# Latent attention over paged keys: pages turned in 32x32 blocks on VectorE, scores on 32-row quarters of TensorE

## The chip, the cores and the metric

One core of a Trainium2 chip runs the whole program. The metric is the device time of one execution in microseconds. Three runs of the kernel before gave 3005.11, 3011.60 and 3019.53; the median is 3011.6. One more execution was recorded by the profiler.

## The reference, cut to what matters

A decoder layer, twice: feed-forward, three mixers side by side (a recurrence, a dilated window attention, a latent attention), feed-forward. 256 prompt tokens and 8 samples of 8 new tokens each pass through it. Everything is float32. The change is in the third mixer, for the samples. Each of them has 2048 past positions in a paged cache of 128 positions a page: 256 latent numbers and 32 rotary numbers a position. 8 heads x 8 tokens make 64 queries a sample, all on the same keys.

```python
def latent_attention(q_lat, q_rope, ckv_all, krope_all, q_off):
    scale = (DNOPE + DROPE) ** -0.5
    ...
        s = (jnp.einsum('bqhc,blc->bhql', ql, ckv_all)
             + jnp.einsum('bqhr,blr->bhql', qr, krope_all)).astype(jnp.float32) * scale
        s = jnp.where(key_rows[None, :] <= rows[:, None], s, -jnp.inf)
        p = jax.nn.softmax(s, axis=-1)
        return jnp.einsum('bhql,blc->bqhc', p.astype(ckv_all.dtype), ckv_all)
```

## The kernel before

The program is written engine by engine, and each engine runs its list in order. Semaphores (`S["..."]`) join the lists. The order around the change is written out by hand in a function `ml_sample` of three engines; nothing schedules it. Transposes have line 654 and matmuls line 651 in the profile, since two helpers issue them.

A sample's pages come by indirect DMAs that GpSimd issues (lines 633 and 636): one for the rotary part (`KRr`) and two for the latent part (`KRc`, 8 positions to a partition in each half). Four buffers hold four samples. Sample 0 is loaded long before; samples 1 to 3 are issued as the stage begins; sample b + 3's are issued when values(b - 1) has raised `ml_pv`.

Positions lie in partitions, which is right for the product with the shares but not for the scores, where channels must lie there. So TensorE turns every 128x128 piece (`transposed`, groups of four), nine groups a sample, into two PSUM banks; ScalarE empties the even ones (line 1626) and VectorE the odd ones (line 2180) into `KTl` and `KRT`. `scores` then contracts 128 channels at a time. The 64 queries fill half of the array's columns, so two halves of the keys go side by side (`r` = 0, 1). `QL` holds the latent queries, `QRz` the rotary ones, four times with zeros around. The scores of a sample fill two PSUM banks, of two pairs that take turns.

Then, per sample: VectorE finds the maximum over PSUM (`maximum`, line 2191 is the large one of 128x1024), ScalarE takes exponentials (`exponentials`, lines 1636 and 1637), TensorE turns the shares (`shares`, 8 pieces of 128x128 and a small one), VectorE copies them out (`shares_out`, lines 2217 and 2218), TensorE multiplies them with the pages (`values`, 8 pairs and a last small product), ScalarE copies the result (line 1647), and `by_channel` turns it while dividing. `own_tokens` scores the 8 new tokens. TensorE's loop weaves these steps of samples b, b - 1 and b - 2 between the transposes of the next half.

`prompt_branch` is the last projection of the prompt's part of this mixer, in 8 tiles with weights ("br", "c") that SP loads when `ml_pv` is 6. Those of `w_out` ("wo") follow. They fill the end of the stage. Before the stage stands `ml_prompt`, which ends with `prompt_y`.

Of the kernel before, what the change touches and what calls it, by code (L numbers as in the profile page):

```python
# [175 lines left out]
TAIL_BANK = (4, 5, 0, 1, 2, 3, 7, 6)  # L176
# [44 lines left out]
def weight_slots(units):  # L221
# [24 lines left out]
    "latent_root", "lora_g", "lora_wa", "lt_T", "lt_act", "lt_dve", "masked", "prods", "q_ev", "series", "state", "t_ev", "vb", "x2_ev", "xp", "y_out", "logs", "mixed", "ml_PT", "ml_done",  # L246
    "ml_exp", "ml_mm", "ml_nm", "ml_oT", "ml_olT", "ml_osb", "ml_own", "ml_div", "ml_p", "ml_prep", "ml_pt", "ml_pv", "ml_s", "ml_yc",
# [8 lines left out]
def build(nc, io):  # L256
    SCB, SCC = DH ** -0.5, (DNOPE + DROPE) ** -0.5
    with ExitStack() as ctx:
# [11 lines left out]
        h = sb("h", KD * T)[:, :].rearrange("p (k t) -> p k t", k=KD)  # L270
# [117 lines left out]
        s_index = sem("page_rows")  # L388
        s_const, s_next = sem("constants"), sem("next_params")
# [5 lines left out]
        cleared_early = [s_par, s_sml, s_out, s_state, s_wkv, s_shin, s_shout] + s_vw + s_kw + [S[n] for n in STEPS if n not in to_the_end]  # L395
# [24 lines left out]

        def latent_out(e):

            return (S["lt_dve"], e // 2 + 1) if e % 2 else (S["lt_act"], e // 2 + 1)

        def evicted(n, e):

            b, a = n // 2, n % 2
            i = e - 9 * b - 4 * a - 1
            return KRT[b % 2] if i < 0 else KTl[n % 2][:, i % 2, i // 2, :]

# [87 lines left out]
        def _(sp):  # L518
# [13 lines left out]
            with sp.Fori(0, DEPTH) as l:  # L532
# [4 lines left out]
                for i, (name, srcs) in enumerate(units):  # L537
# [103 lines left out]
        def _(pe):  # L641
# [552 lines left out]
            def prompt_branch(m):  # L1194
# [3 lines left out]
                if TAIL_BANK[m] == 4:  # L1198
                    pe.wait_ge(S["lt_act"], 9 * NB // 2)
                    pe.wait_ge(S["lt_dve"], 9 * NB // 2)  # L1200
# [8 lines left out]
            def ml_sample():  # L1209
# [5 lines left out]
                def emptied(e):  # L1215

                    if e >= 0:
                        pe.wait_ge(*latent_out(e))

                def transposed(n, g):  # L1220

                    b, a = n // 2, n % 2
                    if b >= NB or g >= 5 - a:
                        return
                    if g == 0:
                        pe.wait_ge(s_kr[b % 4], l * (48 * NB // 4) + 48 * (b // 4 + 1))
                    e = 9 * b + 5 * a + g
                    emptied(e - 2)
                    i = g - 1 + a
                    for t in range(4):  # L1230
                        src = KRr[b % 4][:, t * P:t * P + P] if i < 0 else KRc[b % 4][i % 2][:, 4 * a + t, i // 2 * P:i // 2 * P + P]
                        q = tr(ps[:, 4 + e % 2, t * P:t * P + P], src)
                    q.then_inc(S["lt_T"], 1)

                def scores(n, c):

                    b, a = n // 2, n % 2
                    if b >= NB:
                        return
# [1103 lines left out]
```

## Time and profile before

| | |
|---|---|
| profiled execution | 3013.6 us |
| its span | 3011.7 us |
| TensorE matmuls busy | 2839.3 us (94%), 18716 records |
| VectorE busy | 958.5 us (32%) |
| ScalarE busy | 521.8 us (17%) |
| mean granted clock of TensorE | 0.976 of full speed |
| mean DMA rate | 169 GB/s |

Busy time is what an engine executed; a float32 matmul leaves two records.
### The profile page before, as it was taken

The numbers are of one execution on the slowest core, as the hardware profiler recorded it, in microseconds if no ns is written. First come the engines' busy times: TensorE is split into PE (matmuls) and PEld (weight loads), VectorE is DVE, ScalarE is ACT, GpSimd is POOL, SyncE is SP. The second block draws the span as 40 slices with busy tenths as digits, with TensorE's granted clock in tenths as the row PEclk, the third lists the DMA queues.
The fourth block names the chain that finished last, engine by engine and source line by source line (L and its number), as shares of the span: only waits on it lengthen the run. The fifth ranks groups of instructions, "written<-read, shape, count | busy, mean of one in ns | idle before, by whom it ended". The sixth has DMA issues, their size and how long they took to land.

```text
span 3011.7 us, 44364 instructions
## 1 busy us (share of the span) xinstructions
PE 2839.3 (94%) x18716; PEld 1907.6 (63%) x18716; DVE 958.5 (32%) x2505; ACT 521.8 (17%) x1094; POOL 67.4 (2%) x92
## 2 busy tenths in 40 slices
PE   7999989999999999999899999899998999999997
PEld 5767656656666556776567666565566665567765
DVE  1210444345524432221122104443455244422211
ACT  1000121023411221100010002210334112220000
POOL 0000000000000100000000000000000001000000
PEclk9999999999999999999999999999999999999998
DMA  6434698944931424333523346987458314243344
GB/s 207 133 87 138 217 329 298 319 152 157 356 136 57 158 92 139 107 117 96 159 91 120 98 143 231 333 295 279 151 196 338 116 57 158 92 140 112 115 109 144
DMA packets 263419, 509.69 MB, mean 169 GB/s; under 512 B 9584, under 2 KB 202480, under 8 KB 248112
## 3 DMA queue, kind: packets, MB, share of 16 engines
q1 hardware_dynamic: 254512, 335.35, 33.5%
q0 software_dynamic: 8704, 171.45, 15.7%
q8 instruction: 150, 2.46, 0.3%
q14 instruction: 53, 0.43, 0.0%
HBM read 498.30 MB, written 142.16 MB: 213 GB/s over the span
## 4 chain that ended last, share of the span: by engine, by line
PE 88%; DMA 5%; DVE 3%; ACT 2%; issue 1%; SPq 0%; POOL 0%; DVEq 0%; POOLq 0%; ACTq 0%
PE ps L651 81%; PE ps L654 7%; DMA ring<-in_w_in_dram 2%; DMA big<-in_cache_swa_k_dram 1%; DMA ring<-in_cache_mla_ckv_dram,pidx 1%; DMA ring<-in_f_wu_dram 0%; ACT big L1567 0%; ACT reg L1567 0%; DVE reg L1712 0%; DVE ring L2218 0%; DVE x L1723 0%; DVE reg L2053 0%; DVE ys L2052 0%; DVE ring L2107 0%; DVE big L1917 0%
## 5 line engine op out<-in xcount | busy, mean ns | idle before, releaser
L651 PE MATMUL ps<-h,ring 128*128 128x320 f32 (+1 forms) x3840 | 1076.4, 438 | 44.1 <-ACT h L1422 23.4
L651 PEld LDWEIGHTS ps<-h,ring 128*128 128x128 f32 (+1 forms) x3840 | 725.4, 191 | 350.2 <-issue 40.8
L651 PE MATMUL ps<-big,ring 128*128 128x320 f32 (+3 forms) x2624 | 506.0, 370 | 18.9 <-DVE big L1735 8.1
L651 PEld LDWEIGHTS ps<-big,ring 128*128 128x128 f32 (+2 forms) x2624 | 349.9, 170 | 186.7 <-issue 39.8
L651 PE MATMUL ps<-ring,h 128*128 128x512 f32 (+3 forms) x896 | 252.3, 479 | 8.8 <-DMA ring<-in_w_in_dram 5.8
L1730 DVE TENSOR_TENSOR big<-ps,reg 128x320 f32<-128x320 f32 x88 | 43.2, 491 | 571.5 <-PE ps L651 571.5
L651 PEld LDWEIGHTS ps<-ring,h 128*128 128x128 f32 (+1 forms) x896 | 105.8, 168 | 93.6 <-issue 71.9
L654 PE MATMUL ps<-cst,big 128*128 128x128 f32 x944 | 140.4, 283 | 19.9 <-ACT big L1567 7.3
L1440 ACT ACTIVATE reg<-big 128x320 f32<-128x320 f32 x88 | 41.4, 471 | 659.4 <-DVE big L1730 659.4
L651 PE MATMUL ps<-reg 128*16 128x8 f32 (+13 forms) x1864 | 144.8, 279 | 2.5 <-DVE sml L1986 1.4
L1705 DVE TENSOR_TENSOR h<-h 128x320 f32<-128x320 f32 x36 | 17.7, 492 | 392.3 <-ACT h L1431 392.3
L651 PE MATMUL ps<-ring 128*16 128x128 f32 (+4 forms) x2080 | 128.7, 281 | 12.2 <-DVE ring L2218 8.8
L654 PEld LDWEIGHTS ps<-cst,big 128*128 128x128 f32 x944 | 101.7, 140 | 59.4 <-issue 19.8
L651 PEld LDWEIGHTS ps<-reg 128*16 128x16 f32 (+4 forms) x1864 | 101.8, 128 | 46.7 <-issue 31.6
L651 PE MATMUL ps<-reg,ring 128*128 128x320 f32 (+2 forms) x480 | 118.2, 443 | 7.9 <-DVE reg L2053 4.5
L651 PE MATMUL ps<-ys,ring 128*128 128x320 f32 (+2 forms) x512 | 122.0, 384 | 0.0
L651 PEld LDWEIGHTS ps<-ring 128*16 128x16 f32 (+3 forms) x2080 | 94.6, 117 | 35.3 <-issue 26.0
L651 PEld LDWEIGHTS ps<-reg,ring 128*128 128x128 f32 (+2 forms) x480 | 74.0, 179 | 47.0 <-issue 17.5
L1431 ACT ACTIVATE h<-ps 128x320 f32<-128x320 f32 x48 | 21.0, 437 | 458.8 <-PE ps L651 458.8
L651 PEld LDWEIGHTS ps<-ys,ring 128*128 128x128 f32 x512 | 84.0, 191 | 21.6 <-issue 4.2
L654 PE MATMUL ps<-cst,reg 128*128 128x128 f32 (+1 forms) x516 | 87.5, 284 | 6.6 <-DVE ring L2107 4.2
L654 PEld LDWEIGHTS ps<-cst,reg 128*128 128x128 f32 (+1 forms) x516 | 58.1, 141 | 44.8 <-issue 26.1
(258 smaller groups left out, 2231.7 us busy)
## 6 DMA issues: line engine op xcount, KB each, us to landing
out_o_swa_k_s_dram<-in_cache_swa_k_dram POOLq DMA_DIRECT2D x16, 4080.0 KB, 16.0
out_o_swa_v_s_dram<-in_cache_swa_v_dram POOLq DMA_DIRECT2D x16, 4080.0 KB, 16.1
ring<-in_w_in_dram SPq DMA_DIRECT2D x30, 2048.0 KB, 11.1
ring<-in_f_wg_dram SPq DMA_DIRECT2D x47, 1024.0 KB, 5.3
ring<-in_f_wu_dram SPq DMA_DIRECT2D x47, 1024.0 KB, 7.7
ring<-in_f_wd_dram SPq DMA_DIRECT2D x32, 1408.0 KB, 7.1
big<-in_cache_swa_k_dram SPq DMA_DIRECT2D x32, 1024.0 KB, 8.3
ring<-in_cache_swa_v_dram SPq DMA_DIRECT2D x32, 1024.0 KB, 6.9
```

What stands on the lines that cost most here:

```text
L651: return pe.matmul(out, lhsT, rhs, start=first, stop=last, skip_group_check=True)
L654: return pe.transpose(out, in_, ident[0:rows, 0:rows])
L1431: act.activation(h[:, m, :], ps[:, m % 4, 0:T], ACT.Square, scale=D_MODEL ** -0.5 / half).then_inc(S["down_y"], 1)
L1440: act.activation(sg2[:, m % 2, :], act_t[:, m, :], ACT.Sigmoid).then_inc(S["ffn_sg"], 1)
L1705: q = dve.tensor_tensor(h[:, 0, :], h[:, 0, :], h[:, m, :], ALU.add)
L1730: dve.tensor_tensor(act_t[:, m, :], ps[:, m % 3, 0:T], rstd, ALU.mult).then_inc(S["ffn_t"], 1)
```

## The change

VectorE turns the pages, in blocks of 32x32 from SBUF to SBUF (`turned`, `keys`). A block transpose leaves each quarter of 32 partitions with its own positions: partitions 32i to 32i + 31 hold, for a block of 32 channels, the keys that lay in those same partitions. So each quarter needs all 9 blocks of channels (8 latent, 1 rotary), one after the other, with the queries of that block in its own 32 partitions. `QL` therefore holds the queries in four arrangements: 12 DMAs from SP copy them between partitions (`queries_spread`). `scores` is now 72 matmuls of 32 rows, 64 outputs and 256 columns: 9 blocks x 4 quarters x 2 halves, each quarter into its own PSUM bank. There is one set of these four banks, so the scores of b wait for the exponentials of b - 1. `QR` needs no zeros, and its memset goes. The page copies out of PSUM are gone; `shares_out` moves from VectorE to ScalarE; the shares' banks are 4 and 5, own tokens and by_channel use bank 6. Page buffers move: one half of the fourth now lies in `h`. The first weights of "wo" wait for the last scores instead of the last values. The order of steps on TensorE and VectorE is new.

On TensorE before, part of the loop's step for sample 2: scores of its first half (64x512 and the rotary 64x128), page transposes of its second half (line 654), values of sample 0 (64x256).

```order
L651 MATMUL ps<-big,reg 64x512 [waits lt_dve,lt_act,ml_exp]
L651 MATMUL ps<-big,reg 64x512
L654 MATMUL ps<-cst,ring 128x128 [waits lt_dve]
L654 MATMUL ps<-cst,ring 128x128 x3
L651 MATMUL ps<-big,reg 64x512 x2
L654 MATMUL ps<-cst,reg 128x128 [waits lt_act]
L654 MATMUL ps<-cst,reg 128x128 x3
L651 MATMUL ps<-ring,reg 64x128 x8
L651 MATMUL ps<-ring 64x256 [waits ml_olT,ml_own,ml_pt]
L651 MATMUL ps<-ring 64x256 x7
```

And in the changed kernel, the scores of sample 3 and what follows them, up to the values of sample 2:

```order
L649 MATMUL ps<-ring,reg 64x256 [waits ml_keys,ml_exp]
L649 MATMUL ps<-ring,reg 64x256 x31
L649 MATMUL ps<-big,reg 64x256 [waits ml_keys]
L649 MATMUL ps<-big,reg 64x256 x31
L649 MATMUL ps<-big 64x256 [waits ml_keys]
L649 MATMUL ps<-big 64x256 x7
L649 MATMUL ps<-ring 128x64 [waits ml_olT,ml_own,ml_div,ml_osb]
L649 MATMUL ps<-ring 128x64
L649 MATMUL ps<-reg 64x8 [waits ml_olT,ml_own]
```

The page transposes are gone from TensorE's list, and the scores stand in one piece behind three waits for keys. by_channel (128x64), own tokens (64x8) and the values follow, and behind them the shares' transposes, which wait for the exponentials.

On VectorE, before, around a maximum (line 2180 is a page copy, 2190 to 2195 the maximum, 2201 and 2202 own_share):

```order
L2190 TENSOR_REDUCE sml<-ring 64x1 [waits ml_mm,ml_pt]
L2191 TENSOR_REDUCE sml<-ps 128x1
L2192 COPY sml<-sml 64x1 [waits vector_step]
L2193 TENSOR_REDUCE sml<-sml 64x1 [waits vector_step]
L2194 TENSOR_SCALAR sml<-sml 64x1 [waits vector_step]
L2195 TENSOR_SCALAR sml<-sml 64x1
L2223 COPY reg<-ps 128x16x8 [waits ml_oT,ml_nm]
L2180 COPY ring<-ps 128x512 [waits lt_T,ml_mm,ml_olT]
L2180 COPY ring<-ps 128x512 [waits lt_T,ml_mm]
L2201 MEMSET ring 64x8 [waits ml_exp]
```

In the changed kernel, from the end of the maximum of sample 3 to the divisor (2138 is own_scores, 2171 the result, 2156 and 2157 own_share, 2162 the divisor's first):

```order
L2138 TENSOR_TENSOR ring<-ps,cst 64x8 [waits ml_s,ml_nm]
L2171 COPY reg<-ps 128x16x8 [waits ml_oT,ml_own]
L2116 STREAM_TRANSPOSE big<-ring 128x4x256 [waits ml_mm,ml_olT]
L2116 STREAM_TRANSPOSE big<-h 128x4x256
L2116 STREAM_TRANSPOSE big<-h 128x512
L2156 MEMSET ring 64x8 [waits ml_PT,ml_exp]
L2157 COPY ring<-ring 64x8
L2116 STREAM_TRANSPOSE ring<-big 128x4x256 [waits ml_mm,pages_in_0]
L2116 STREAM_TRANSPOSE ring<-big 128x4x256
L2162 COPY sml<-sml 64x1
```

Five block transposes a sample stand there, two of them behind a wait for pages, ahead of the next maximum.

```diff
-        QRz = reg[:, 2016:2016 + 2048].rearrange("p (i b n) -> p i b n", i=4, b=NB)
+        QR = big[:, 2560:2560 + 512].rearrange("p (b n) -> p b n", b=NB)
...
-        Pown = ring[0:NS, 12056:12056 + TS]
-        kr_at = [(big, 3072, big, 5120, big, 7168), (ring, 0, ring, 2048, ring, 4096), (reg, 8672, reg, 10720, reg, 12768), (reg, 13280, ring, 9088, ring, 11136)]
+        Pown = [ring[0:NS, 12056 + TS * i:12056 + TS * i + TS] for i in range(2)]
+        kr_at = [(big, 3072, big, 5120, big, 7168), (ring, 0, ring, 2048, ring, 4096), (reg, 10720, reg, 12768, reg, 14816),
+                 (ring, 9088, h_flat, 0, h_flat, 2048)]
...
-        QL = reg[:, 15328:15328 + 1024].rearrange("p (c b n) -> p c b n", c=2, b=NB)
-        KTl = [buf[:, at:at + 2048].rearrange("p (s c k) -> p s c k", s=2, c=2) for buf, at in ((big, 0), (ring, 4608))]
-        KRT = [ring[:, 6656 + 512 * i:7168 + 512 * i] for i in range(2)]
-        Pl = big[:, 2048:2048 + 1024]
-        PTL = cut(ring, 7680, 8, P)
+        QL = reg[:, 2016:15328].rearrange("p (c n) -> p c n", c=2)
+        KTl = [cut(ring, 4608 + 2048 * i, 4, 512) for i in range(2)]
+        KTh, KRT = cut(big, 0, 4, 512), big[:, 2048:2048 + 512]
+        Pl = reg[:, 15328:15328 + 1024]
+        PTL = cut(reg, 0, 8, P)
...
                     if name == ("br", "c"):
+                        sp.wait_ge(S["ql_ev"], 1)
+                        for to in range(4):
+                            for turn in range(1, 4):
+                                at = 32 * ((to + turn) % 4)
+                                sp.dma_start(QL[32 * to:32 * to + 32, :, 512 * turn:512 * turn + 512], QL[at:at + 32, :, 0:512]).then_inc(s_ql, 16)
                         sp.wait_ge(S["ml_pv"], 6)
                     if name == ("wo", 0):
-                        sp.wait_ge(S["ml_pv"], NB)
+                        sp.wait_ge(S["ml_mm"], NB)
                     if name == ("wo", 1):
                         sp.wait_ge(S["ml_olT"], NB)
...
+                pe.wait_ge(s_ql, 16 * 12)
+
+                def scores(b):
+
+                    if b:
+                        pe.wait_ge(S["ml_exp"], b)
+                    for d in range(9):
+                        if d in (0, 4, 8):
+                            pe.wait_ge(S["ml_keys"], 5 * b + {0: 2, 4: 4, 8: 5}[d])
+                        kt = KTl[b % 2][:, d, :] if d < 4 else KTh[:, d - 4, :] if d < 8 else KRT
+                        for i in range(4):
+                            rows = slice(32 * i, 32 * i + 32)
+                            at = 512 * ((d - i) % 4) + NS * b
+                            queries = QL[rows, d // 4, at:at + NS] if d < 8 else QR[rows, b, :]
+                            for r in range(2):
+                                q = mm(ps[64 * r:64 * r + NS, i, 0:256], queries, kt[rows, 256 * r:256 * r + 256], d == 0, d == 8)
+                    q.then_inc(S["ml_mm"], 1)
...
+                own_tokens(0)
+                for b in range(NB):
+                    scores(b)
                     by_channel(b - 2)
+                    own_tokens(b + 1)
+                    values(b - 1)
+                    for r in range(2):
+                        shares(b, r)
+                by_channel(NB - 2)
+                prompt_branch(0)
+                prompt_branch(1)
+                values(NB - 1)
                 prompt_branch(2)
-                values(NB - 1, 0)
-                values(NB - 1, 1)
                 prompt_branch(3)
...
-                    pair = ps[:, 2 * (b % 2):2 * (b % 2) + 2, :]
...
+                    act.activation(Pl.rearrange("p (u i k) -> p i u k", u=8, i=4), ps[:, 0:4, 0:256].rearrange("p i (u k) -> p i u k", u=8),
+                                   ACT.Exp, scale=SCC, bias=sml[:, 4:5], accum_out=sml[:, 8:9])
...
+                def shares_out(b, r):
+                    act.wait_ge(S["ml_PT"], 2 * b + r + 1)
+                    if r:
+                        act.activation(PTl, ps[0:NS, 7, 448:512], ACT.Copy)
+                    act.activation(PTL[:, 4 * r:4 * r + 4, :], ps[:, 4 + r, :].rearrange("p (t n) -> p t n", t=4), ACT.Copy).then_inc(S["ml_pt"], 1)
+
+                for b in range(NB):
+                    exponentials(b)
+                    output(b - 1)
+                    for r in range(2):
+                        shares_out(b, r)
+                output(NB - 1)
...
-                link(dve.memset(QRz, 0.0))
...
+                def turned(out, pages):
+                    dve.transpose(out, pages).then_inc(S["ml_keys"], 1)
+
+                def keys(b, high):
+
+                    if b >= NB:
                         return
+                    if high:
+                        dve.wait_ge(S["ml_mm"], b) if b else None
+                    else:
+                        dve.wait_ge(s_kr[b % 4], l * (48 * NB // 4) + 48 * (b // 4 + 1))
+                        if b >= 2:
+                            dve.wait_ge(S["ml_mm"], b - 1)
+                    for r in range(2):
+                        out = (KTh if high else KTl[b % 2])[:, :, 256 * r:256 * r + 256].rearrange("p d (u k) -> p d u k", u=8)
+                        turned(out, KRc[b % 4][r][:, :, P * high:P * high + P].rearrange("p u (d k) -> p d u k", d=4))
+                    if high:
+                        turned(KRT, KRr[b % 4])
...
+                dve.wait_ge(S["pgm"], 24)
+                dve.wait_ge(S["gate"], 24)
+                for high in range(2):
+                    keys(0, high)
+                own_scores(0)
+                for b in range(NB):
+                    keys(b + 1, 0)
                     if b:
                         divisor(b - 1)
...
+                    maximum(b)
+                    own_scores(b + 1)
+                    if b >= 2:
+                        result(b - 2)
+                    keys(b + 1, 1)
+                    own_share(b)
+                divisor(NB - 1)
```

## Rows read from the trace of the kernel before

**Rows 1.** The chain that ended last, its shares of the span by engine.
```profile
PE 88%; DMA 5%; DVE 3%; ACT 2%; issue 1%; SPq 0%; POOL 0%; DVEq 0%; POOLq 0%; ACTq 0%
```

**Rows 2.** Line 2191: duration ns min/median/max, first and last start; then VectorE's timeline.
```profile
L2191 DVE TENSOR_REDUCE sml<-ps x16: 1205/1206/1208, 1000.3 to 2619.9; 128x1 f32<-128x1024 f32 x16
...
1119.28 1.21 DVE L2191 TENSOR_REDUCE sml<-ps 128x1 f32<-128x1024 f32 x1
...
2500.95 1.21 DVE L2191 TENSOR_REDUCE sml<-ps 128x1 f32<-128x1024 f32 x1
```

**Rows 3.** Window: length, busy (count) of PE, PEld, DVE, ACT, POOL, clock, DMA, GB/s.
```profile
1048.60:1067.30 18.70, 18.16 (x142) 11.09 (x143) 8.04 (x24) 4.42 (x10) 2.82 (x3) 1.00 0.40 143
```

**Rows 4.** TensorE's timeline in the stage: start, length, line, shapes, count.
```profile
996.84 1.09 PE L654 MATMUL ps<-cst,ring 128*128 128x128 f32 x8
997.87 1.09 PE L651 MATMUL ps<-ring,reg 128*64 128x128 f32 x16
...
1048.66 0.63 PE L651 MATMUL ps<-ring 128*128 128x64 f32 x4 [0.41 <-DVE ring L2218]
...
1050.68 0.66 PE L654 MATMUL ps<-cst,big 128*128 128x128 f32 x4
1051.26 1.08 PE L651 MATMUL ps<-big,reg 128*64 128x512 f32 x4
...
1053.78 1.90 PE L651 MATMUL ps<-reg,ring 128*64 128x256 f32 x16
1055.61 0.66 PE L654 MATMUL ps<-cst,big 128*128 128x128 f32 x4
1056.19 2.52 PE L651 MATMUL ps<-reg,ring 128*64 128x256 f32 x18
1058.64 0.66 PE L654 MATMUL ps<-cst,ring 128*128 128x128 f32 x4
1059.23 0.61 PE L651 MATMUL ps<-reg 128*64 128x8 f32 x6
1059.77 1.08 PE L651 MATMUL ps<-ring,reg 128*64 128x512 f32 x4
```

**Rows 5.** TensorE's timeline in two other stages, and a window of the recurrence.
```profile
466.96 0.63 PE L651 MATMUL ps<-cst,big 64*64 64x64 f32 x16
467.42 0.63 PE L651 MATMUL ps<-cst,reg 64*64 64x64 f32 x16
...
753.48 2.37 PE L651 MATMUL ps<-ring 128*16 128x128 f32 x80
```
```profile
2087.00:2088.00 1.00, 1.00 (x42) 1.00 (x38) 0.00 (x0) 0.00 (x0) 0.00 (x0) 1.00 1.95 653
```

**Rows 6.** VectorE's copies, by line; ScalarE's timeline at the first exponentials.
```profile
L2180 DVE COPY ring<-ps x40: 691/692/693, 987.6 to 2611.2; 128x512 f32<-128x512 f32 x40
...
L2163 DVE COPY reg<-reg x8: 414/417/420, 903.5 to 2403.6; 32x512 f32<-32x512 f32 x8
...
1002.27 1.11 ACT L1636 ACTIVATE big<-ps,sml 128x1024 f32<-128x1024 f32 x1 [1.60 <-DVE sml L2195]
...
1003.57 0.19 ACT L1637 ACTIVATION_READ_ACCUMULATOR ring<-ring,sml 64x1 f32 x1
```

**Rows 7.** SP's last gate weights, the first wait for pages, landing of line 636.
```profile
913.23 22.79 SPq L577 DMA_DIRECT2D ring<-in_w_in_dram  x2
...
993.12 0.66 PE L654 MATMUL ps<-cst,ring 128*128 128x128 f32 x4 [0.79 <-DMA ring<-in_cache_mla_ckv_dram,pidx]
...
DMA to landing us min/median/max: 5.7/7.9/11.5
```

**Rows 8.** The end of the stage: values(6), a window of it, the results' projection.
```profile
1121.66 6.93 PE L651 MATMUL ps<-reg,ring 128*64 128x256 f32 x34 [1.72 <-DVE reg L2223]
...
1127.00:1128.00 1.00, 1.00 (x11) 0.44 (x7) 0.00 (x0) 0.00 (x0) 0.00 (x0) 0.94 0.00 0
...
1144.97 0.34 PE L651 MATMUL ps<-reg 128*64 128x64 f32 x4
```

More of the change, by code:

```diff
@@ L394, in build @@
                       "down_y", "x")
-        cleared_early = [s_par, s_sml, s_out, s_state, s_wkv, s_shin, s_shout] + s_vw + s_kw + [S[n] for n in STEPS if n not in to_the_end]
+        cleared_early = [s_ql, s_par, s_sml, s_out, s_state, s_wkv, s_shin, s_shout] + s_vw + s_kw + [S[n] for n in STEPS if n not in to_the_end]
         cleared_last = [s_dve] + s_slot + [S[n] for n in to_the_end] + [s_out]
@@ L1213, in ml_sample @@
                 pe.wait_ge(S["br_ev"], 2 * KD)
[L1215 to L1239, printed above, removed]
-                    if c == 0:
-                        if a == 0 and b >= 2:
-                            pe.wait_ge(S["ml_exp"], b - 1)
-                        done = 9 * b + 5 + 4 * a
-                        pe.wait_ge(S["lt_act"], (done + 1) // 2)
-                        pe.wait_ge(S["lt_dve"], done // 2)
-                    bank = 2 * (b % 2) + a
-                    o = lambda r, at, w: ps[64 * r:64 * r + NS, bank, at:at + w]
-                    if c < 2:
-                        for r in range(2):
-                            mm(o(r, 0, 512), QL[:, c, b, :], KTl[n % 2][:, r, c, :], c == 0, False)
-                        return
-                    for i in range(4):
-                        for r in range(2):
-                            q = mm(o(r, i * P, P), QRz[:, i, b, :], KRT[b % 2][:, (2 * r + a) * P:(2 * r + a) * P + P], False, i == 3)
+                pe.wait_ge(s_ql, 16 * 12)
@@ L1273, in shares @@
                         pe.wait_ge(S["ml_exp"], b + 1)
-                        pe.wait_ge(S["ml_p"], b + 1)
-                    if b or r:
-                        pe.wait_ge(S["ml_pt"], 2 * b + r)
-                    for u in range(4):
-                        q = tr(ps[:, 6, u * P:u * P + P], Pl[:, (4 * r + u) * P:(4 * r + u) * P + P])
-                    if r:
-                        pe.wait_ge(S["ml_own"], min(b + 2, NB))
+                    if b:
+                        pe.wait_ge(S["ml_pt"], 2 * b - 1 + r)
+                    for u in range(4):
+                        q = tr(ps[:, 4 + r, u * P:u * P + P], Pl[:, (4 * r + u) * P:(4 * r + u) * P + P])
+                    if r:
+                        pe.wait_ge(S["ml_p"], b + 1)
                         if b:
@@ L1284, in shares, with values @@
                     q.then_inc(S["ml_PT"], 1)
-                def values(b, part):
-                    if not 0 <= b < NB:
+                def values(b):
+                    if b < 0:
                         return
-                    if part == 0:
-                        pe.wait_ge(S["ml_pt"], 2 * b + 2)
-                        pe.wait_ge(S["ml_own"], min(b + 2, NB))
-                        if b:
-                            pe.wait_ge(S["ml_olT"], b)
+                    pe.wait_ge(S["ml_pt"], 2 * b + 2)
+                    if b:
+                        pe.wait_ge(S["ml_osb"], b)
                     o = lambda r: ps[64 * r:64 * r + NS, 7, 0:KV_LORA]
-                    for u in range(4 * part, 4 * part + 4):
+                    for u in range(8):
                         for r in range(2):
                             mm(o(r), PTL[:, u, 64 * r:64 * r + NS], KRc[b % 4][r][:, u, :], u == 0, r == 1 and u == 7)
-                    if part:
-                        mm(o(0), PTl, PBc[0:NS, 2, Q_LORA:Q_LORA + KV_LORA], False, True).then_inc(S["ml_pv"], 1)
+                    mm(o(0), PTl, PBc[0:NS, 2, Q_LORA:Q_LORA + KV_LORA], False, True).then_inc(S["ml_pv"], 1)
                 def by_channel(b):
@@ L1616, in ml_sample @@
             def ml_sample():
-                def pages_out(n, after=None):
-                    b, a = n // 2, n % 2
-                    first = 9 * b + 5 * a
-                    if n >= 2:
-                        act.wait_ge(S["ml_mm"], n - 1)
-                    for e in range(first + first % 2, first + 5 - a, 2):
-                        act.wait_ge(S["lt_T"], e + 1)
-                        act.activation(evicted(n, e), ps[:, 4, :], ACT.Copy).then_inc(S["lt_act"], 1)
-                        if after is not None and e < first + 2:
-                            exponentials(after)
                 def exponentials(b):
```

145 lines of the change are left out of this document (37 added, 108 removed).

## The prediction, as it was written before the changed kernel ran

> **What bounds the kernel now.** I read the chain of waits first: 88% of the span is TensorE's [rows 1]. In the stage that the change touches, the samples' latent attention, it is the same. Its clock tick is the large maximum at line 2191, once per sample, 16 times in two layers. Call its start T(b) for sample b. In layer 1 T(0) is 1000.3 and T(7) 1119.3, in layer 2 2500.95 and 2619.9: 119.0 us each, 17.0 a sample; the first interval, without values, is shorter, and a full one is 18.1 as a mean of two parities. [rows 2] The window of such a sample has PE busy 18.16 of 18.70 us at a granted clock of 1.00, VectorE 8.04, ScalarE 4.42 [rows 3]. So only TensorE's list decides, and what is taken from it is time, as long as nobody else becomes the bound.
>
> In TensorE's rows start to start is the cost, since the last 0.16 us of each row is the drain [rows 4]. A group of four page transposes takes 0.58 us (1050.68 to 1051.26), nine groups a sample: 5.2 us. They go, and so do the old score products. What stays: by_channel 0.47 (0.63 less the drain), own tokens 0.54 (1059.23 to 1059.77), values 1.83 and 2.45, which joined save one turn of the array's shape of about 0.16, so 4.12; eight share transposes 1.02 (996.84 to 997.86) and the small one, about 0.23. Sum kept 6.38 us; the old scores and a stall are the rest, 18.1 - 6.4 - 5.2 = 6.5.
>
> **The new scores.** 72 matmuls of 32 rows, 64 outputs, 256 columns; a matmul leaves two records, so 144. The values at 1053.78 have 16 records of 256 columns in 1.83 us, two column halves side by side [rows 4]: 0.213 us for a step of two. One quarter and half alone would need 144 x 0.213 = 30.7 us; the two halves together 15.4 (as the values show); eight tiles at once 3.84. No row shows quarters of the array. Nearest are the 64-row halves: 16 records of 64x64 in 0.46 us, 29 ns each, where 64 columns alone take a quarter of 0.213, 53 ns: two row halves do run at once [rows 5]. Four column quarters do too: 80 records of 128 columns in 2.37 - 0.16 us, 27.6 ns against 107 alone [rows 5]. Weight loads have a floor: 42 records a microsecond of 64 weights and 16 columns, 24 ns [rows 5]; 144 of these are 3.4 us, under the 3.84. I take 29 ns, the row with weights and columns equally tight: 4.17, and 0.16 for the turn, S = 4.3 us. Bounds 4.0 and 15.5.
>
> A page sets it lower. The Trainium skill ("TensorE: Matmul & The Clock Gate", section "Part 3: Packing small matmuls — row/col tiling") has four row tiles giving 3.07 times, not four. By it S would be 144 x 0.213 / 6.14 = 5.0 and the time 2919; no row here has four row tiles, and the two-way row gives 1.84 of 2.
>
> So a full sample costs TensorE 6.4 + 4.3 = 10.7 us.
>
> **Who else could bound.** VectorE: the copies of pages (4.5 of 0.69 us [rows 6]) and three share copies (1.6) go; of 8.04 busy [rows 3] 3.4 stay, with the gaps of their chains 3.9. New are four 32x32-block transposes of 1024 elements and one of 512 a sample. No row has one. A copy within SBUF of 512 elements takes 0.42, from PSUM 0.69, and 1024 elements through the maximum 1.21 [rows 2, 6]. Bounds: at the SBUF copy's pace about 0.7 each, 3.2 us a sample; at half the PSUM pace 2.3 each, 10.4. I take the maximum's, since a block must be filled before it is drained: 4 x 1.21 + 0.69 = 5.5, VectorE 9.4 of 10.7. Covered, by 1.3 us.
>
> The chain from scores to shares: maximum to ScalarE's start 1.97 us (1000.3 to 1002.27), exponentials to the last read 1.49 (to 1003.76) [rows 2, 6], 3.5 in all. Scores now have one set of banks, so the next scores wait for it. It lies under by_channel, own tokens and values (5.1). The high half of the next keys follows the maximum, own scores and result: 2.4 + 3.1 = 5.5, and then own_share, 5.8, waited for by the small share transpose at about 6.1. Just covered. Share copies on ScalarE (1.5 us) lie under the next scores.
>
> Pages: sample b+3's loads go when values(b-1) ends, 5.1 after T(b); three issues 1.25 apart, the last landing 7.9 later (5.7 to 11.5) [rows 7], so at 15.8; VectorE asks for them at 10.7 + 5.8 = 16.5. Covered by 0.7, and another 1.3 before the maximum slips.
>
> The spread queries: SP is free for 12 DMAs once the last gate weights are issued, near 936 (913.23 + 22.79), and the stage starts at 983: hidden [rows 7]. The memset that goes is of an earlier stage, where TensorE has gate tiles to do; I count nothing for it. w_branch_c goes when values(5) ends, T(7) - 5.6, and is wanted at T(7) + 6.3; even the slowest page load takes 11.5 [rows 7], so it is hidden, narrowly at worst.
>
> **The start.** VectorE's first keys begin as the stage does, at 983, and take 5.5, scores(0) run behind them and end near 989.9. But VectorE turns the low half of sample 1 before maximum(0), and these pages land at 993.1 [rows 7]. So T(0) = 993.1 + 2.5 + 0.1 = 995.7. Exponentials end at 999.2, keys(1) and own_share at 1001.2, scores(1) start at 1001.5. TensorE has then idled some 9 us. Idle lowers its clock: after the idle before 1121.66 the granted clock was at the lower level of 1.2 GHz (34 records in 6.93 us, 0.43 a step of two, twice 0.213), and it was back at 2.4 within 1127 to 1128, some 5.5 us after work resumed [rows 8]. So half clock until 1004.7, which costs 1.6: T(1) = 1001.5 + 4.3 + 1.6 = 1007.4. Then T(7) = 1007.4 + 6 x 10.7 - 0.5 (no by_channel in the first) = 1071.1, against 1119.3: 48.2 earlier.
>
> **The end.** Before, values(6) ran at half clock after waiting for a result, and the projection of the results began at 1145.0, T(7) + 25.7 [rows 8]. Now: 0.5 + 4.1 + 1.25 + 0.5, two branch tiles 3.8, values(7) 4.1, two tiles 3.8, by_channel 0.4, one tile 1.9: T(7) + 20.3. 5.4 more.
>
> **Sum.** 48.2 + 5.4 = 53.6 a layer, 107 in two. The profiled execution took 3013.6 us with span 3011.7; 3013.6 - 107 = 2906. The median of the runs, 3011.6, lies 2 below it, inside their 3005 to 3020; I stay at 2906.
>
> **Rivals.**
> Row quarters don't overlap, only the column halves. Then S = 15.5, the sample 21.9, T(1) 1018.6, T(7) 1149.5: 30.2 later, less 5.4, 25 a layer: 3063, slower. T(7) is 1041.0 + 7 S (S once in T(1), six times after), so it decides above S = (1119.3 + 5.4 - 1041.0) / 7 = 12.0. For it: four row groups writing four banks at once is in no row. Against: the 64-row halves at 29 ns. 10%.
> Two of four quarters overlap: S = 7.85, sample 14.2, T(7) 1095.7, 29 a layer: 2956. 12%.
> Block transposes at half pace: VectorE 10.4 + 3.9 = 14.3 a sample, T(1) 1011.6, T(7) 1097.4: 2959. Against: nothing but that the trace has no row; for: four-byte elements through a 32x32 block. 12%.
> Pages late: two samples can't be shorter than 5.1 + 0.3 + landing + 3.4 + 0.1. With 10.4 that is 9.7 a sample, with the slowest landing (14.0) 11.5; at 18, as if other traffic shared the engines, 13.5: T(7) 1088, 2940. 7%.
> Forecast 54%, own range 2893 to 2922 (S from 4.0 to 5.3, the 29 ns a quarter worse, and a start some 3 us off). 5% for what I don't see, half of it slower.
>
> The range 2890 to 2963 takes in all but the first rival and the rest. A measurement of this kernel can tell about 0.5%, 15 us, from no change. Faster 0.86, same 0.03, slower 0.11.
>
> **What would show it.** Scores of a sample: one row of 144 records, 4.2 to 4.5 us; near 8 or 15.5 names the rival. STREAM_TRANSPOSE of 128x1024 at 1.2 us; 2.3 is the other. T(b) to T(b+1) 10.7 with PE busy over 95%; idle of PE before the small share transpose or before the scores' fifth block would say VectorE is the bound, VectorE idle for pages that loads are. T(0) near 995.7 and a granted clock of 0.50 around 1001 to 1004 for the start. I am wrong if T(7) - T(1) is outside 60 to 70 us.

## The result, and the profile after

| | before | after |
|---|---|---|
| median of the runs, us | 3008.4 (3004.4 to 3019.5) | 2897.6 (2893.1 to 2909.1) |
| ratio to before, 95% interval | | 0.963 (0.959 to 0.967) |
| profiled execution, us: time, span | 3013.6, 3011.7 | 2909.1, 2907.5 |
| granted clock of TensorE, mean | 0.976 | 0.970 |
| PE busy, DVE busy, us | 2839.3, 958.5 | 2734.8, 968.1 |

The changed kernel is faster by 3.7%. The median before has a fourth run in it, so it is 3008.4 here and not the 3011.6 of the prediction. Timed again later it stood at 0.964 (0.958 to 0.969). The kernel before was timed again beside each set of experiments, with medians between 3013 and 3028 us, so the experiments are compared by ratio.

The chain of waits of the changed kernel, its shares by engine, has hardly moved against [rows 1]:

```profile
PE 89%; DMA 4%; DVE 3%; ACT 2%; issue 1%; POOL 0%; SPq 0%; DVEq 0%; POOLq 0%; ACTq 0%
```

VectorE's timeline at the stage's clock tick, the large maximum, now line 2145 (start, length, what it is, and the idle time before it with what ended it), answers to [rows 2]:

```profile
997.32 1.20 DVE L2145 TENSOR_REDUCE sml<-ps 128x1 f32<-128x1024 f32 x1
...
1008.57 1.23 DVE L2145 TENSOR_REDUCE sml<-ps 128x1 f32<-128x1024 f32 x1 [2.48 <-PE ps L649]
1018.52 1.22 DVE L2145 TENSOR_REDUCE sml<-ps 128x1 f32<-128x1024 f32 x1 [1.13 <-PE ps L649]
...
1071.36 1.22 DVE L2145 TENSOR_REDUCE sml<-ps 128x1 f32<-128x1024 f32 x1 [3.81 <-PE ps L649]
...
2518.74 1.23 DVE L2145 TENSOR_REDUCE sml<-ps 128x1 f32<-128x1024 f32 x1 [3.82 <-PE ps L649]
```

T(7) - T(1) is 62.8 us. The first interval lacks by_channel (9.95), the other five are 10.57 each; before, the same six were 15.9 to 18.7, and the full ones 18.69 and 17.42 by turns, 18.1 in the mean. The idle time in brackets ends with TensorE: at the maximum VectorE waits for it and not the other way round. The window of one sample (columns as in [rows 3]), and one at the start of the stage:

```profile
1039.65:1050.22 10.57, 10.57 (x199) 7.62 (x199) 8.70 (x20) 3.17 (x8) 2.82 (x3) 1.00 0.64 221
1000.80:1004.60 3.80, 3.79 (x41) 2.84 (x49) 3.77 (x5) 1.30 (x3) 0.00 (x0) 0.50 0.99 419
```

TensorE is busy 10.57 of 10.57 at a granted clock of 1.00. VectorE has 8.70 of it. The second window lies behind TensorE's idle time at the start: its clock is 0.50 there, and the DMA engines are full (0.99), as the pages of samples 1 to 3 still arrive. TensorE's timeline in the stage (start, length, line, shapes, count) shows the new list, against [rows 4]:

```profile
984.74 0.37 PE L649 MATMUL ps<-reg 128*64 128x8 f32 x4 [0.77 <-issue]
...
1000.81 1.97 PE L652 MATMUL ps<-cst,reg 128*128 128x128 f32 x8 [8.42 <-ACT ring L1575]
1002.71 0.13 PEld L652 LDWEIGHTS ps<-cst,ring 64*64 64x64 f32 x1 [0.33 <-DVE ring L2157]
1002.95 3.33 PE L649 MATMUL ps<-ring,reg 32*64 32x256 f32 x64
...
1044.78 1.09 PE L652 MATMUL ps<-cst,reg 128*128 128x128 f32 x8
1045.80 0.24 PE L652 MATMUL ps<-cst,ring 64*64 64x64 f32 x1
1045.97 1.98 PE L649 MATMUL ps<-ring,reg 32*64 32x256 f32 x64
1047.75 1.93 PE L649 MATMUL ps<-big,reg 32*64 32x256 f32 x64
1049.48 0.64 PE L649 MATMUL ps<-big 32*64 32x256 f32 x16
1050.04 0.66 PE L649 MATMUL ps<-ring 128*128 128x64 f32 x4
```

The scores are 144 records from 1045.97 to 1050.04: S = 4.07 us. The old scores took 5.98, start to start: four groups like the one at 1051.26 of [rows 4], 1.01 each, and two rotary groups of 0.92 and 1.02, the first of them here:

```profile
1052.27 0.65 PE L654 MATMUL ps<-cst,big 128*128 128x128 f32 x4
1052.86 1.09 PE L651 MATMUL ps<-ring,reg 128*64 128x128 f32 x16
```
So a full sample is shorter by 18.06 - 10.57 = 7.5 us: 5.2 are the page transposes, 1.9 the scores, and some 0.4 the idle time that TensorE had between its steps before. The four quarters do not make the scores much shorter than they were; they keep them short although they now contract only 32 rows at a time.

A stage is read from its first to its last step: from 984.74 to the projection of the results at 1091.28 it takes 106.5 us in layer 1, where it took 161.6 (983.42 to 1144.97 [rows 8]); in layer 2 106.6 (2431.99 to 2538.63) for 161.0. That is 55.0 and 54.4, 109.4 together. The two spans differ by 104.2, so some 5 us of it are lost in other stages of these two executions. The medians differ by 110.8.

VectorE's block transposes, line 2116, at the start of the stage; the last of the three rows starts when the pages of sample 1 have landed [rows 7]:

```profile
984.76 2.37 DVE L2116 STREAM_TRANSPOSE ring<-big 128x1024 f32<-128x1024 f32 x2 [2.21 <-ACT ys L1497]
987.05 2.92 DVE L2116 STREAM_TRANSPOSE big<-big 128x1024 f32<-128x1024 f32 x3
...
994.99 2.37 DVE L2116 STREAM_TRANSPOSE ring<-ring 128x1024 f32<-128x1024 f32 x2 [4.83 <-DMA ring<-in_cache_mla_ckv_dram,pidx]
```
Landing of the page loads of line 634 (us from the start of an issue, least, median, most):

```profile
DMA to landing us min/median/max: 6.2/7.3/8.3
```
This list has only the loads whose arrivals the trace holds completely, 8 of 32 (those of samples 1 and 5). The others show in VectorE's timeline, as waits in front of the low half of the next keys. In layer 2, for samples 4 and 6 (at 2493.70 no releaser is named, but the last arrival of these pages is recorded at 2493.62):

```profile
2471.97 2.37 DVE L2116 STREAM_TRANSPOSE ring<-big 128x1024 f32<-128x1024 f32 x2 [0.76 <-DMA big<-in_cache_mla_ckv_dram,pidx]
2476.24 1.23 DVE L2145 TENSOR_REDUCE sml<-ps 128x1 f32<-128x1024 f32 x1 [0.69 <-PE ps L649]
...
2493.70 2.37 DVE L2116 STREAM_TRANSPOSE ring<-reg 128x1024 f32<-128x1024 f32 x2 [1.12 <-issue]
2497.61 1.22 DVE L2145 TENSOR_REDUCE sml<-ps 128x1 f32<-128x1024 f32 x1 [0.33 <-PE ps L649]
```
The last loads of these samples were issued at 2463.07 and 2484.20, so the waits end 8.9 and 9.5 us later. Nothing is lost by it, since VectorE still comes to the maximum before the scores are done, but of its 1.4 us of room 0.7 and 0.3 are left.

The projection of the results:

```profile
1091.28 0.34 PE L649 MATMUL ps<-reg 128*64 128x64 f32 x4
```

### The profile page after: what moved, and what is told of

Read it like the earlier page. It is cut to its first block, busy times and chain, and to the rows that moved or that the text cites. A ratio compares the mean times of both kernels' runs of the same rounds, so it can differ in the third digit from the quotient of the medians.

```text
span 2907.5 us, 46136 instructions
## 1 busy us (share of the span) xinstructions
PE 2734.8 (94%) x19676; PEld 1866.1 (64%) x19676; DVE 968.1 (33%) x2463; ACT 500.2 (17%) x1070; POOL 67.2 (2%) x92
## 4 chain that ended last, share of the span: by engine, by line
PE 89%; DMA 4%; DVE 3%; ACT 2%; issue 1%; POOL 0%; SPq 0%; DVEq 0%; POOLq 0%; ACTq 0%
PE ps L649 84%; PE ps L652 5%; DMA ring<-in_w_in_dram 3%; DMA big<-in_cache_swa_k_dram 1%; DMA ring<-in_f_wu_dram 1%; DMA ring<-in_cache_mla_ckv_dram,pidx 1%; ACT big L1517 0%; ACT reg L1517 0%; DVE reg L1657 0%; DVE x L1668 0%; DVE reg L1998 0%; DVE ys L1997 0%; DVE ring L2052 0%; DVE big L1862 0%; DVE ring L2116 0%
## 5 line engine op out<-in xcount | busy, mean ns | idle before, releaser
L649 PE MATMUL ps<-big,ring 128*128 128x320 f32 (+2 forms) x2496 | 498.5, 374 | 18.9 <-DVE big L1680 8.1
L649 PEld LDWEIGHTS ps<-big,ring 128*128 128x128 f32 (+1 forms) x2496 | 346.5, 174 | 185.4 <-issue 44.8
L649 PE MATMUL ps<-ring,h 128*128 128x512 f32 (+3 forms) x896 | 252.9, 479 | 14.6 <-DMA ring<-in_w_in_dram 9.4
L649 PE MATMUL ps<-reg 128*16 128x8 f32 (+14 forms) x1960 | 153.6, 285 | 3.3 <-DVE sml L1931 1.7
L1650 DVE TENSOR_TENSOR h<-h 128x320 f32<-128x320 f32 x36 | 17.7, 492 | 392.7 <-ACT h L1381 392.7
L652 PE MATMUL ps<-cst,big 128*128 128x128 f32 (+1 forms) x672 | 98.2, 283 | 16.7 <-ACT big L1517 7.3
L649 PE MATMUL ps<-ring 128*16 128x128 f32 (+3 forms) x1888 | 99.2, 272 | 3.4 <-DVE ring L2052 3.4
L652 PEld LDWEIGHTS ps<-cst,big 128*128 128x128 f32 (+1 forms) x672 | 72.1, 140 | 37.2 <-ACT big L1517 12.4
L652 PE MATMUL ps<-cst,reg 128*128 128x128 f32 (+3 forms) x436 | 73.6, 288 | 23.3 <-ACT ring L1575 16.6
L649 PE MATMUL ps<-reg,ring 128*128 128x320 f32 (+1 forms) x288 | 83.1, 444 | 4.5 <-DVE reg L1998 4.5
L649 PE MATMUL ps<-ring,reg 32*64 32x256 f32 (+2 forms) x1312 | 81.2, 395 | 3.7 <-DVE ring L2116 3.7
L649 PE MATMUL ps<-big,reg 32*64 32x256 f32 (+7 forms) x1792 | 81.0, 355 | 1.2 <-issue 0.7
```

What stands on the lines that cost most here:

```text
L649: return pe.matmul(out, lhsT, rhs, start=first, stop=last, skip_group_check=True)
L652: return pe.transpose(out, in_, ident[0:rows, 0:rows])
L1650: q = dve.tensor_tensor(h[:, 0, :], h[:, 0, :], h[:, m, :], ALU.add)
```

## The experiments

The theory: TensorE's list sets the stage; the page transposes that it lost are worth 5.2 us a sample, the overlap of the four row quarters keeps the new scores at 4.07 us, and VectorE with 5.3 us of transposes stays just under TensorE. The rivals: the gain comes from elsewhere (the share copies on ScalarE, the order of steps), or VectorE is the bound already.

**Only the page transposes.** The kernel before, with three of the four transposes of each group left out:
```
-                    for t in range(4):
+                    for t in range(3, 4):
```

> The kernel before, with three of four page transposes of each group left out (the scores then use stale numbers); the copies out of PSUM and all waits stay. It measures what the transposes on TensorE were worth. Theory: TensorE's list bounds, 27 transposes of 0.107 us less a sample, 18.1 to 15.2, 46 us in all, 2962. Rival: the copies of ScalarE and VectorE (0.60 and 0.69 each, two banks in turn) bound the groups once these are short: T(b) to T(b+1) over 16.5, 25 us or less in all, 2983.

Measured: 2982.6 us against 3028.5, ratio 0.985 (0.981 to 0.989), 46 us less in the medians, 34 to 58 by the interval. The row of a page group shows what went: one transpose in 0.26 us where four took 0.58, so 9 x 0.32 = 2.9 us a sample.

```profile
1036.28 0.33 PE L654 MATMUL ps<-cst,big 128*128 128x128 f32 x1
1036.54 1.08 PE L651 MATMUL ps<-ring,reg 128*64 128x512 f32 x4
```
The intervals did not shrink by as much. In layer 1 T(1) is at 1009.98 and T(7) at 1103.67, 15.6 us a sample for 17.7. The same full sample, first before and then here:

```profile
1084.74:1103.43 18.69, 18.17 (x142) 11.10 (x143) 8.04 (x24) 4.40 (x10) 0.00 (x0) 1.00 0.07 27
...
1072.71:1089.09 16.38, 15.32 (x115) 8.48 (x115) 8.10 (x24) 4.14 (x9) 0.00 (x0) 1.00 0.14 57
```
```profile
1088.53 0.63 PE L651 MATMUL ps<-ring 128*128 128x64 f32 x4 [0.81 <-DVE ring L2218]
```
TensorE is busy 2.85 us less, as the rows say, but the sample is 2.3 us shorter: its idle time grew from 0.5 to 1.1 us, most of it in the wait for VectorE's share copies that the last row shows. So what leaves TensorE's list is time for the most part, here four fifths of it, and not one for one. The stage is 15.5 and 13.2 us shorter in the two layers of the profiled execution, 29 together; what the rest of the 46 is, no run shows. The rival was right in part: other engines bound the groups a little. In the changed kernel these gaps are gone, and the share copies lie on ScalarE.

**The quarters one after the other.** The same matmuls; the loop over the quarters goes outside:
```
+                    for quarters in ((0,), (1,), (2,), (3,)):
+                      for d in range(9):
...
-                        for i in range(4):
+                        for i in quarters:
```

> The changed kernel with the 72 score matmuls of a sample issued quarter by quarter (all nine blocks of quarter 0, then of quarter 1, ...) in place of round robin; same instructions, same work. Theory: matmuls on different 32-row quarters run at once, and the order that alternates them is what lets them. Then here only the two column halves overlap: scores 15.5 us a sample in place of 4.07, T(b) to T(b+1) 22.0 in place of 10.57, about 83 us a layer later, 3064 us. Rival: TensorE looks ahead far enough, or the order plays no part: 10.6 a sample and 2898. Second rival: the gain of the change came mostly from the transposes that left TensorE, and the scores cost the same either way: under 2920.

Measured: 3235.2 us against 3028.5, ratio 1.068 (1.064 to 1.073), and 31.9 us a sample. The direction is the theory's, the size is not: windows of the run (columns as above) show the clock, over one sample and in two pieces of its scores:

```profile
1074.16:1106.05 31.89, 31.89 (x198) 18.86 (x198) 8.70 (x21) 3.16 (x8) 2.83 (x3) 0.61 0.21 75
...
1082.00:1086.00 4.00, 4.00 (x35) 2.65 (x35) 1.29 (x7) 1.68 (x4) 2.79 (x3) 1.00 0.46 96
1094.00:1098.00 4.00, 4.00 (x20) 2.10 (x20) 0.00 (x0) 0.00 (x0) 0.00 (x0) 0.50 0.00 0
```
TensorE is busy without a gap, and still the granted clock falls to 0.50 (1.2 GHz) in the lone quarters and stays there into the next values. The first quarter, still at full clock, takes 3.84 us (1083.46 to 1087.30), and four of these are the 15.4 us that the prediction has for two column halves alone. The third starts here and the fourth 6.04 us later:

```profile
1093.35 2.34 PE L649 MATMUL ps<-ring,reg 32*64 32x256 f32 x10
...
1099.39 2.34 PE L649 MATMUL ps<-ring,reg 32*64 32x256 f32 x10
```
That is less than twice 3.84. An estimate from the mean clock: 31.89 us at 0.61 are 19.5 us at full clock, under the 22.0 that I expected, and the other 12.4 are the clock. Where one quarter follows another, the rows of both run side by side for a while, which may be the difference; that was not tried apart.

**Pairs of quarters.** The same with `((0, 1), (2, 3))`.

> The changed kernel with quarters 0 and 1 alternating, then 2 and 3. Theory: overlap is in proportion to the quarters that alternate: scores 7.9 us a sample, T(b) to T(b+1) 14.3, 26 us a layer later, 2951. Rival: overlap needs only a neighbour on other rows and the queue does the rest: under 11.5 a sample, 2915. Rival: overlap comes with all four only: 22 a sample, 3064.

Measured: 2990.2 us against 3028.5, ratio 0.988 (0.984 to 0.992). Behind the first two, samples are 14.4 us, and 13.64 in the two without page loads. In one of the latter the clock stays up:

```profile
1099.86:1113.50 13.64, 13.64 (x198) 9.36 (x199) 6.32 (x18) 3.17 (x8) 0.00 (x0) 1.00 0.43 155
```
Its scores run from 1106.22 to 1113.36, 7.14 us: two at once take 1.75 times the 4.07 of four at once. Overlap of the quarters is thus what makes the new scores cheap; in both runs only the order of issue was changed.

**Every block transpose twice.**
```
                 def turned(out, pages):
+                    link(dve.transpose(out, pages))
                     dve.transpose(out, pages).then_inc(S["ml_keys"], 1)
```

> The changed kernel with each block transpose on VectorE done twice, one after the other. Theory: VectorE has 10.57 less about 9.6 us of slack a sample; with 5.3 us more it is the bound at about 15.0 a sample, T(7) some 32 later in a layer, 2963, with TensorE idle some 4 us a sample. Rival: the transposes are hidden and have much room: 2898 to 2910.

Measured: 2981.0 us against 3018.1, ratio 0.987 (0.984 to 0.989); samples of 14.6 to 16.2 us in layer 1. In a sample VectorE is now full, and TensorE has a gap of 4.29 us in front of the small share transpose, where it waits for own_share:

```profile
1081.12:1096.11 14.99, 10.70 (x185) 7.33 (x181) 14.36 (x27) 3.16 (x8) 0.00 (x0) 0.89 0.01 3
```
```profile
1090.00 0.24 PE L652 MATMUL ps<-cst,ring 64*64 64x64 f32 x1 [4.29 <-DVE ring L2158]
```
This is nearly the third rival of the prediction (transposes at half pace, 14.3 a sample, ratio 2959 / 3013.6 = 0.982), which was priced a little low: the bound does change over, and costs over 4 us a sample.

**Fewer scores.** Four of the nine blocks of the keys are left out of the scores:
```
-                    for d in range(9):
+                    for d in (0, 1, 4, 5, 8):
```

> The changed kernel with four of the nine channel blocks left out of the scores (the result is then not the reference's). Scores 80 records, about 2.3 us. Theory: TensorE's list would take 8.8 us a sample, but VectorE's, with 8.7 busy and its waits, takes 9.4 to 9.6, and becomes the bound: 16 us less in all, 2882, VectorE without a wait for TensorE before the maximum. Rival: TensorE alone counts: 8.8 a sample, 25 us less, 2873. Rival: page loads bound: 9.3, with VectorE waiting for them.

Measured: 2896.3 us against 3018.1, ratio 0.960 (0.957 to 0.962), near the changed kernel's 0.963. 64 records of 144 should give back 1.8 us a sample and a sample of 8.8. From T(1) to T(6) the mean is 9.23. A window over two samples, the second of them alone, and VectorE's rows of the first:

```profile
1034.33:1053.07 18.74, 17.98 (x271) 12.36 (x269) 17.21 (x41) 6.33 (x16) 2.82 (x3) 1.00 0.57 216
```
```profile
1044.01:1053.07 9.06, 8.29 (x130) 5.63 (x126) 8.60 (x21) 3.16 (x8) 0.00 (x0) 1.00 0.44 184
```
```profile
1040.50 2.37 DVE L2116 STREAM_TRANSPOSE ring<-reg 128x1024 f32<-128x1024 f32 x2 [0.65 <-DVE ring L2157]
...
1044.01 1.21 DVE L2145 TENSOR_REDUCE sml<-ps 128x1 f32<-128x1024 f32 x1
```
The maximum follows on without idle time in front, so VectorE is the bound. The two samples differ: 9.06 us where VectorE waits for nothing, 9.68 where it waits 0.65 in front of the low half of the keys. The wait is put down to VectorE's own copy, long done; what its list has at this place is the wait for pages, whose last arrival is recorded at 1040.42. VectorE's own list is thus 9.06 us and not the predicted 9.4, and its room under the changed kernel's 10.57 is 1.5 and not 1.3; late pages take up part of it, so the rival that waits for loads is right in part. T(7) - T(1) is 54.4 us for 62.8 in layer 1 and 54.1 for 63.0 in layer 2, 17.3 less together where 16 were forecast; the ratios show about 11, with an uncertainty as large.

**The share copies back on VectorE.** The copies are moved, in VectorE's order behind own_share:
```
+                    for r in range(2):
+                        shares_out(b, r)
                 divisor(NB - 1)
```

> The changed kernel with the copies of the turned shares back on VectorE, behind own_share. Theory: VectorE's chain a sample becomes 5.8 to own_share, then it waits for the share transposes, copies until 7.6, keys 10.0, divisor 11.0, maximum 11.2: 0.6 more than 10.57, 9 us in all, 2906. Rival: VectorE has the room (8.7 busy + 1.6 is under 10.57): 2898, no difference.

Measured: 2906.6 us against 3018.1, ratio 0.964 (0.961 to 0.966), the changed kernel's own. A window of one sample:

```profile
1039.21:1050.18 10.97, 10.97 (x201) 7.97 (x201) 10.13 (x24) 1.87 (x5) 2.82 (x3) 1.00 0.57 200
```
VectorE has 10.13 of 10.97, and samples are 10.1 to 11.0 (mean 10.63, where the changed kernel has 10.47 over the same six). In most of them the maximum follows without idle time in front, so VectorE is the bound there, as expected, but by less than the 0.6 us expected. That is 2 us in two layers, too little for the medians. TensorE counts as busy 10.97 of 10.97 all the same, for a list of 10.57: the busy share alone does not tell who bounds. Moving these copies was hardly part of the gain; it bought room.

**The first maximum first.** TensorE idles 8.4 us at the start, since VectorE waits for the pages of sample 1 before maximum(0). Here maximum(0) and own_share(0) come before that wait:
```
-                    keys(b + 1, 0)
+                    if b:
+                        keys(b + 1, 0)
...
+                    if b == 0:
+                        own_share(0)
+                        keys(1, 0)
```

> The changed kernel with VectorE's first step in another order: maximum of sample 0, own_share of 0, then the keys of sample 1, so that the wait for the pages of sample 1 no longer holds up the exponentials of sample 0. Theory: the idle of TensorE at the start (8.4 us) is on the path and its clock with it: T(0) 991.9 in place of 997.3, T(1) about 1002.7 in place of 1008.6, 5.9 a layer, 12 in all, 2886. Rival: the pages of sample 1 (landing at 995.0) and the ten keys' transposes behind them bound scores(1) anyway: under 3 us in all, 2895 or more.

Measured: 2935.6 us against 3028.5, ratio 0.970 (0.967 to 0.973). A miss: not faster than the changed kernel, and samples that overlap page loads took 12.65 us. TensorE's timeline in one of them shows 53 records in 3.05 us where 64 take 1.98, and then a gap that no wait explains; the window has the clock at full height:

```profile
1048.91 3.05 PE L649 MATMUL ps<-ring,reg 32*64 32x256 f32 x53
1052.24 0.52 PE L649 MATMUL ps<-ring,reg 32*64 32x256 f32 x6 [0.28 <-issue]
```
```profile
1042.52:1055.17 12.65, 12.21 (x198) 8.31 (x198) 8.72 (x20) 3.17 (x8) 2.82 (x3) 1.00 0.54 183
```
Was it the order, or this loading of the kernel, or the chip? The changed kernel had not been timed beside it. Both kernels ran again, side by side, on another chip.

> The changed kernel itself, as a control beside the next two. If the samples of 12.65 us in the run that took the first maximum first came from its order on VectorE, this run has none: 10.57 us a sample again and a ratio of 0.963. If they came from that chip or that loading, this run can show them too, and its ratio goes to 0.970.

> The run that took the first maximum first, once more. There the scores of a sample that overlapped page loads took 6.1 us in place of 4.1: the last rounds of the first 64 records came at 0.71 us for four. If that belongs to the order, it comes again: 12.65 us in samples 2 to 5, 10.6 in those without loads, ratio 0.970. If it was of that one run, the samples are at 10.6 and the ratio falls to 0.957, since the start of the stage is then 9 us shorter in each layer.

Measured: the changed kernel 2906.0 us against 3012.7, ratio 0.964 (0.958 to 0.969), 10.57 a sample; the other one 2907.6, ratio 0.962 (0.956 to 0.968). In its second run the scores are as they should be:

```profile
1036.63 1.98 PE L649 MATMUL ps<-ring,reg 32*64 32x256 f32 x64
1038.41 1.93 PE L649 MATMUL ps<-big,reg 32*64 32x256 f32 x64
```
So the order alone does not make the slow rounds. Whether they belonged to that loading or to that chip stays open: the pairs of quarters ran on the same chip and were 0.75 us longer in the samples with page loads. What they were stays open too. And the 9 us a layer that I hoped for are only 3 to 4. Stage start to T(0) falls from 12.6 to 7.2 us. But scores(1) need the pages of sample 1 too: VectorE's timeline has them behind maximum(0), five transposes in a row.

```profile
1000.24 2.37 DVE L2116 STREAM_TRANSPOSE ring<-ring 128x1024 f32<-128x1024 f32 x2
1002.53 2.92 DVE L2116 STREAM_TRANSPOSE big<-ring 128x1024 f32<-128x1024 f32 x3
```
From the stage's start (989.27 there) T(1) comes after 19.8 us for 23.8, T(7) after 83.4 for 86.6, and in layer 2 after 83.0 for 86.8. Some 7 us in two layers are 0.2%, less than the intervals can tell.

**Page loads later.** On top of it, the loads of samples 4 to 7 wait for one more set of scores:
```
                         pool.wait_ge(S["ml_pv"], b - 3)
+                        pool.wait_ge(S["ml_mm"], b - 1)
```

> The first maximum first, and in addition GpSimd issues the pages of samples 4 to 7 only after the scores that followed in its neighbour (some 5 us later), so that the transfers start behind the scores and not under them. If the slow rounds come from transfers that start under the scores, the samples 2 to 5 fall from 12.65 to 10.6 us and the ratio to 0.964. If the transfers have no part in it, the samples stay at 12.65 and the ratio at 0.970. The pages are still in time: 8 us of landing against some 16 of room.

Measured: 2915.7 us against 3012.7, ratio 0.967 (0.961 to 0.973). It could no longer tell about the slow rounds, which its neighbour did not have either. It shows something else: my own "still in time" was wrong. Samples became 14.9 and 14.1 us long, for VectorE waited 5.7 us for pages at 1027.61. Their last load was issued at 1019.64 and so landed 8.0 later:

```profile
1027.61 2.37 DVE L2117 STREAM_TRANSPOSE ring<-big 128x1024 f32<-128x1024 f32 x2 [5.67 <-DMA big<-in_cache_mla_ckv_dram,pidx]
```
A delay of some 5 us is more than the cover, as the prediction's own 0.7 + 1.3 us says, and the changed kernel had used up part of that already. The rival of late pages was near.

## Why the prediction was right, step by step

Predicted 2906 (own range 2893 to 2922); measured 2909 in the profiled execution, 2898 in the median.

- **TensorE is the bound, and what leaves its list is time.** Right in the changed kernel: busy 10.57 of 10.57, and VectorE waits for it at each maximum. In the kernel before it holds for the most part: the run without three of four transposes gained 2.3 us a full sample of the 2.9 that its rows say. Some of the gain of the change is that these gaps closed as well.
- **Scores S = 4.3 us, from 29 ns a record.** Measured 4.07: 144 records at 28 ns with the turn of the shape in it. Eight tiles at once would be 3.84. By the Trainium skill ("TensorE: Matmul & The Clock Gate", section "Part 3: Packing small matmuls — row/col tiling") four row tiles give 3.07 times, and S would be 5.0 by that estimate (the 2919 us given for it are 2916 by the prediction's own sum). The trace does not agree: from the 15.4 us of two column halves to 4.07 is 3.8 times.
- **Kept list 6.38.** Measured 10.57 - 4.07 = 6.50. by_channel is the most of it: 0.59 for 0.47, now that rows of another shape follow it. The prediction took 0.16 us off each row for the drain; most rows of [rows 4] give 0.07 (1.08 long, 1.01 to the next), without harm to the sum, which goes from start to start.
- **Sample 10.7.** Measured 10.57: the two errors of 0.2 and 0.1 took each other back in part.
- **Block transposes 5.5 us, at the pace of the maximum.** Measured 2.37 + 2.96 = 5.33 us. 1024 elements take 1.20 to 1.25 us. The list of VectorE is 9.1 and not 9.4, as the run with fewer scores shows.
- **Own share just under the small share transpose.** Right for a full sample (no gap of TensorE at 1045.80). In the first, with nothing above it, the weight load at 1002.71 waits 0.33 for it, without making the matmul later than the clock does.
- **Pages land 7.9 after the issue, needed 0.7 later.** Wrong by a little. The last load of sample 6 was to land 15.8 us after T(3), 0.7 before VectorE asks for it. VectorE had to wait for it until 16.8 (1029.09 to 1045.88), 0.69 us, and in layer 2 up to 1.12 us: the waits end 8.8 to 9.5 after the last issue. The 1.3 us in front of the maximum took this up. The result came out right by that reserve and not by the landing time. The late loads confirm how narrow it is.
- **The start.** T(0) 995.7 predicted, 997.32 measured, but the stage began 1.3 later (983.42, 984.74). TensorE idled 8.4 (some 9 predicted) and came back at clock 0.50, which held into the window here, whose mean is 0.65:

```profile
1005.20:1006.00 0.80, 0.80 (x32) 0.58 (x24) 0.66 (x5) 0.00 (x0) 0.00 (x0) 0.65 0.07 31
```

  From the share transposes at 1000.81 to T(1) it took 7.76; the same piece at 1044.78 takes 5.44: 2.3 us of half clock. The 1.6 predicted counted the scores only; the share transposes in front of them pay too (1.97 us for 1.09). T(1) is 1008.57 for 1007.4. That T(7) is 1071.36 for 1071.1 is partly luck: a later start and the clock cost 1.2 us, and six shorter samples gave 0.9 back.
- **The end.** T(7) to the projection 19.9, predicted 20.3: values(6) is at full clock.
- **The sum.** 53.6 a layer predicted, 55.0 and 54.4 measured. The span shows 104 of the 109, the medians 111 of the predicted 107.
- **The rivals.** The one on the other side was priced wrongly: quarters one after the other would have given a ratio of 1.068 and not 3063 / 3013.6 = 1.016, since I left the clock at its upper level. Two at once (2956) would have been about right in the sample (14.4, predicted 14.2), though 0.988 in the ratio for 0.981, its first two intervals being longer: 19.7 and 15.9 us, the first of them wholly at clock 0.50 as its window shows.

```profile
1007.43:1027.15 19.72, 17.01 (x161) 10.40 (x161) 8.36 (x18) 2.78 (x7) 0.00 (x0) 0.50 0.01 2
```

So the low clock after the idle start lasted longer there than the 5 us or so that the changed kernel's start shows. That was in no rival's price.

Not tried apart: the memset that went, the twelve DMAs of the spread queries and the later w_branch_c. None shows as a wait of TensorE in the stage. Nor was the new order of steps tried alone; by the rows of a full sample, transposes and scores account for 7.1 of its 7.5 us, and all else for the rest.

## What to carry to other kernels

Where an engine is busy without a gap, price a change by the rows of its list, start to start, and then give every other engine and every load its own sum per period: here VectorE has 9.1 against 10.6, and the pages come up to 1.1 us late within that room. Look at the idle time in front of the step where the engines meet, and not at busy shares, for who is the bound. Issue matmuls on small tiles round robin over the tiles; the same matmuls tile by tile made a sample of 10.6 us one of 31.9. A step moved ahead of a wait pays only until the next step needs the same data.

## What I had not expected of the hardware

TensorE's granted clock fell from 1.00 to 0.50 while it was busy without a gap, in a run of matmuls on one 32-row quarter with two column halves; with two quarters at once it stayed at 1.00 once it was up (13.64 us window), but came up only in the second sample, where the changed kernel's is up within the first scores behind the idle time. And in one run of one kernel the scores that overlapped page loads lost 2.1 us a sample at full clock, which a second run of the same kernel did not show; in the pairs of quarters, samples with loads were 0.75 us longer than those without; in the changed kernel one sample of all those with loads was longer, by 0.2 us (10.80 in layer 2).
